# Two input tiles of expert 16 in a place of their own, and the output biases' products inside expert 0

## The chip, the cores and the metric

One core of one Trainium2 chip. The metric is the device time in microseconds (us) of one execution of the whole program, the median over several runs.

## The reference

Two blocks run in a row on 256 tokens of width 1024, all in fp32. The first (two layers of convolution, latent attention and dilated attention) and the attention of the second are untouched by the change. The second block ends in a mixture of experts, and this is what the change touches:

```python
logits = xt @ w_router + b_router
top_val, top_idx = lax.top_k(logits, TOP_K)          # 4 of 32 experts for each token
gates = softmax(top_val)
# for each expert e and the tokens that chose it:
hcat = xb @ w_in[e] + b_in[e]                        # 1024 x 2048
x_glu = minimum(hcat[:, :D_FF], 7.0)
x_lin = clip(hcat[:, D_FF:], -7.0, 7.0)
act = x_glu * sigmoid(1.702 * x_glu) * (x_lin + 1)
ys = act @ w_out[e] + b_out[e]                       # 1024 x 1024
# y[token] += gate * ys; then x + gt2 * y, and a last rms_norm
```

Each expert has 8 MB of input weights and 4 MB of output weights, and every expert's are read.

## The kernel before

**Stages.** The core runs the first block's two layers, then the second block's attention ("the block" below), then its output projection, the router, and the experts. Programs of the engines are written out by hand and meet in semaphores; each engine takes its own instructions in order, and every transfer is issued by SyncE (SP), in order, in `block_sync`.

**The ring.** Weights pass through a ring of six slots of 2 MB in SBUF. Each expert fills all six: tiles 0 to 3 are its input weights, 4 and 5 its output weights. Expert 0's are fetched during the block (4, 5, 3, 0 early; 1 and 2 once the last output projection unit is done). `expert(e, m)` in SP's loop over experts 1 to 31 refills a slot when TensorE has used the tile of the expert before: `mused` counts tiles 0, 1, 2 and 4, `lin_done` tile 3, `eout_done` tile 5 (L604 to L615). So up to six tiles are on their way.

**Between block and experts.** On VectorE (DVE): L1276 adds the output projection to x; L1286 clears seven buffers (`bin_sb`, `pos`, `ext`, `ys`, `spread`, `sel`, `selg`); `modulated` (L1132 to L1148) normalizes; then the router's choice, gates and places in each expert's list (L1291 to L1319); `select` (L1329) makes the one-hot matrices `sel` that gather the tokens of experts 0 and 1; then the job table (L1339 to L1355), a list of experts with more tokens than 64 slots, which is used only behind expert 31; and in each turn of the loop over pairs (L1391 on) first `onehots` (L1361, picks the expert's row of the input biases) and `gates_of` (L1368, gate masks). On TensorE (PE): sums of squares L812, router L819, four groups of transpositions of h to token order L830, places L835 to L839, gates turned L843, then eight products of the output biases and the gates into the four accumulating banks (L851), which wait for both bias tables (`bpar_loaded`), and `gather` of expert 0's and 1's tokens (L858) in two halves.

**The experts.** TensorE loops over 16 pairs of experts. For each of the two: `expert_in` (L869: products with tiles 0 to 3, and behind tile 1 the input bias L887), `turn_act` (L913), `expert_out` (L904: tiles 4, 5). In the pair's first expert eight `scatter` products (L927) add the pair before's rows into the banks, six ahead of `turn_act` and two behind; in the first pair they add zeros, as `ys` and `spread` were cleared. `turn_sel` (L920) turns the gate masks. In the pair's second expert the next pair's tokens are gathered. ScalarE (ACT) copies gathered and turned tiles out of PSUM (L1074, L1087, L1079); DVE clips and multiplies (L1375 to L1383) and copies the rows (L1388, L1389).

## Time and profile before

| | us |
|---|---|
| three runs | 2038.09, 2039.31, 2044.0 |
| median | 2039.31 |
| the profiled execution | 2037.97 |
| its span | 2036.2 |

| engine | busy us | share of the span |
|---|---|---|
| PE (TensorE, matmuls) | 1904.2 | 94% |
| DVE | 759.7 | 37% |
| ACT | 546.9 | 27% |
| POOL | 522.6 | 26% |

The mean rate of the DMA engines is 277 GB/s over the span; 563.19 MB are moved. A matmul record's end is modelled, so a busy PE is not PE at its peak, and a product in fp32 leaves two records. "Granted clock" is TensorE's clock as a share of its higher level: 1.00 is 2.4 GHz, 0.50 is 1.2 GHz. In a timeline, what stands in brackets behind a row is the engine's idle time ahead of it and what ended that.

### The profile page before, as it was taken

What the parts mean: (1) busy time and instruction counts of PE and PEld (TensorE: products, weight loads), DVE (VectorE), ACT (ScalarE), POOL (GpSimd) and SP (SyncE); (2) the same over time, 40 slices, a digit from 0 to 9 for tenths busy, and PEclk for the clock granted to TensorE, in tenths of its full rate; (3) what the DMA queues carried; (4) which work ended last, traced back from release to release, by engine and by line L of the source; (5) the groups of instructions that cost most, each with busy time, mean ns of one, the idle gap of its engine ahead of it and who ended that gap; (6) DMA issues with size and microseconds to landing.
All of it is one profiled execution on the core that took longest, in us unless ns stands there. A gap on an engine that the chain in (4) does not pass through costs nothing.

```text
span 2036.2 us, 26901 instructions
## 1 busy us (share of the span) xinstructions
PE 1904.2 (94%) x10970; PEld 1199.2 (59%) x10970; DVE 759.7 (37%) x1445; ACT 546.9 (27%) x922; POOL 522.6 (26%) x220
## 2 busy tenths in 40 slices
PE   7999999989999999799879999999999999999996
PEld 6779889977798899544465444333333333333433
DVE  4784643448836533734544111111111111111112
ACT  4554455445544554222411000000000000000001
POOL 5776656866755567000000000000000000000000
PEclk9999999999999999899998999999999999999999
DMA  8555333565543335421725999999999999999994
GB/s 297 200 183 176 125 125 125 172 231 176 201 150 130 120 125 189 158 75 42 287 93 208 430 428 428 430 428 429 428 428 429 428 428 429 429 429 428 428 429 193
DMA packets 111407, 563.19 MB, mean 277 GB/s; under 512 B 4768, under 2 KB 24352, under 8 KB 86464
## 3 DMA queue, kind: packets, MB, share of 16 engines
q1 hardware_dynamic: 111328, 562.09, 69.1%
q8 instruction: 56, 0.92, 0.2%
q14 instruction: 23, 0.19, 0.0%
HBM read 561.02 MB, written 1.05 MB: 276 GB/s over the span
## 4 chain that ended last, share of the span: by engine, by line
PE 57%; DMA 31%; DVE 7%; ACT 2%; issue 1%; SPq 0%; DVEq 0%; ACTq 0%
DMA ring<-in_e_in_dram 31%; PE bank L1595 14%; PE bank L1585 10%; PE score L869 9%; PE bank L695 4%; PE bank L1562 3%; PE mixed L904 2%; PE bank L802 1%; PE mixed L1679 1%; PE flip L1662 1%; DVE ring L2164 1%; PE score L1648 1%; PE flip L1620 1%; PE bank L927 1%; PE score L887 1%
## 5 line engine op out<-in xcount | busy, mean ns | idle before, releaser
L1971 POOL TENSOR_TENSOR w_lo<-ring,w_hi 128x1024 fp32r<-128x1024 f32 (+1 forms) x216 | 522.4, 2430 | 285.2 <-ACT w_hi L1873 284.6
L869 PE MATMUL score<-ring,space 128*64 128x512 f32 x2048 | 461.4, 595 | 46.2 <-DMA ring<-in_e_in_dram 45.2
L869 PEld LDWEIGHTS score<-ring,space 128*64 128x64 f32 x2048 | 142.3, 137 | 353.9 <-issue 246.2
L1873 ACT ACTIVATE w_hi<-ring 128x1024 fp32r<-128x1024 f32 (+1 forms) x216 | 226.3, 1049 | 221.5 <-PE bank L1595 122.5
L1595 PE MATMUL bank<-h_hi,w_hi 128*128 128x256 f32 x896 | 261.9, 292 | 0.0
L1595 PE MATMUL bank<-h_lo,w_hi 128*128 128x256 f32 x896 | 254.3, 284 | 0.0
L1595 PE MATMUL bank<-h_hi,w_lo 128*128 128x256 f32 x896 | 254.2, 284 | 0.0
L904 PE MATMUL mixed<-ring,space 128*64 128x512 f32 x1024 | 226.8, 595 | 0.0
L1083 ACT ACTIVATE space<-space 128x512 f32<-128x512 f32 x32 | 20.2, 631 | 718.9 <-DVE space L1375 718.9
L1375 DVE TENSOR_SCALAR space<-score 128x512 f32<-128x512 f32 x32 | 22.2, 694 | 431.7 <-PE score L869 431.7
L1595 PEld LDWEIGHTS bank<-h_hi,w_hi 128*128 128x128 f32 x896 | 172.8, 193 | 4.5 <-issue 4.4
L1595 PEld LDWEIGHTS bank<-h_lo,w_hi 128*128 128x128 f32 x896 | 172.7, 193 | 0.1
L1595 PEld LDWEIGHTS bank<-h_hi,w_lo 128*128 128x128 f32 x896 | 172.4, 192 | 0.0
L904 PEld LDWEIGHTS mixed<-ring,space 128*64 128x64 f32 x1024 | 70.7, 137 | 132.6 <-issue 130.6
L1585 PE MATMUL bank<-w_hi,h_hi 128*128 128x512 f32 (+1 forms) x320 | 131.4, 411 | 8.3 <-DVE h_lo L2027 8.3
L1388 DVE COPY space<-mixed 64x512 f32<-64x512 f32 x32 | 21.9, 685 | 295.6 <-PE mixed L904 295.6
L1585 PE MATMUL bank<-w_hi,h_lo 128*128 128x512 f32 (+1 forms) x320 | 124.9, 390 | 0.0
L1585 PE MATMUL bank<-w_lo,h_hi 128*128 128x512 f32 (+1 forms) x320 | 124.6, 389 | 0.0
L1585 PEld LDWEIGHTS bank<-w_hi,h_hi 128*128 128x128 f32 x320 | 61.0, 191 | 25.6 <-issue 12.5
L695 PE MATMUL bank<-ring,h 128*128 128x512 f32 (+1 forms) x160 | 66.6, 569 | 5.1 <-DVE h L1148 5.1
L1585 PEld LDWEIGHTS bank<-w_lo,h_hi 128*128 128x128 f32 x320 | 61.2, 191 | 11.7 <-issue 1.0
L1585 PEld LDWEIGHTS bank<-w_hi,h_lo 128*128 128x128 f32 x320 | 60.9, 190 | 12.0
(320 smaller groups left out, 2330.7 us busy)
## 6 DMA issues: line engine op xcount, KB each, us to landing
ring<-in_e_in_dram SPq DMA_DIRECT2D x128, 2048.0 KB, 25.2
ring<-in_e_out_dram SPq DMA_DIRECT2D x64, 2048.0 KB, 22.1
ring<-in_w_in_dram SPq DMA_DIRECT2D x42, 2048.0 KB, 7.8
ring<-in_w_ada_dram SPq DMA_DIRECT2D x16, 1024.0 KB, 5.4
ring<-in_w_o_dram SPq DMA_DIRECT2D x6, 2048.0 KB, 7.9
ring<-in_w_qkv_dram SPq DMA_DIRECT2D x4, 2048.0 KB, 9.9
ring<-in_w_ada_dram SPq DMA_DIRECT2D x4, 2048.0 KB, 8.0
ring<-in_w_out_a_dram SPq DMA_DIRECT2D x2, 2048.0 KB, 7.7
```

The source lines that it names most:

```text
L695: ins = pe.matmul(b[:, 0:n], src[:, c, tt * P:(tt + 1) * P], w8[:, c, 0:n], start=c == 0, stop=c == DC - 1)
L802: ins = pe.matmul(b[:, i * T:(i + 1) * T], w8[:, c, m:m + P], mix[:, c, :], start=c == 0 and i == 0, stop=c == DC - 1, skip_group_check=True)
L869: ins = pe.matmul(score[HALF * blk:HALF * blk + HALF, which * W:(which + 1) * W], xs[:, 2 * j + r, HALF * hh:HALF * hh + HALF], wk[:, blk ...
L887: pe.matmul(score[HALF * blk:HALF * blk + HALF, which * W:(which + 1) * W], onehot[:, hh, :], bin_sb[:, at:at + W], start=False, stop=False)
L904: ins = pe.matmul(mixed[HALF * side:HALF * side + HALF, :], actT[:, hh, a * P + HALF * half:a * P + HALF * half + HALF], ring[:, 4 + half, ...
L1375: dve.tensor_scalar(glu[:, hh, :], score[:, 0:W], GLU_LIMIT, None, ALU.min).then_inc(glu_free, 1)
L1388: dve.tensor_copy(ys[0:HALF, hh, :], mixed[0:HALF, :])
L1562: ins = pe.matmul(b[:, i * T:(i + 1) * T], w_[:, c, m], y_[br][:, c, :], start=c == 0 and i == 0 and y_ is y_hi and w_ is hi, stop=c == 3 ...
L1585: ins = pe.matmul(b[:, 0:n], x_[:, c, t], w_[:, k % PARTS, i, 0:n], start=c == 0 and x_ is h_hi and w_ is w_hi, stop=c == DC - 1 and x_ is ...
L1595: ins = pe.matmul(b[:, half * T:(half + 1) * T], w_[:, k % PARTS, i, m:m + P], x_[:, c, :], start=c == 0 and half == 0 and x_ is h_hi and ...
L1873: act.activation(split_part(w_hi, k), raw_part(k), ACT.Copy).then_inc(hi_done, 1)
L1971: pool.tensor_tensor(split_part(w_lo, k), raw_part(k), split_part(w_hi, k), ALU.subtract).then_inc(lo_done, 1)
```

## The change

Three things change. Line numbers are those of the kernel before.

1. **Parked tiles.** A place of two tiles (`parked_tiles`) is laid over h and the first 6144 columns of the work space. The buffers of the block and of the experts are moved so that nothing in use lies there. SP fetches tile 1 of expert 16 (the seventeenth) into it behind the last output projection unit, and tile 0 behind the fourth group of transpositions of h (L830), which reads h last. For expert 16 SP issues only tiles 2 to 5, and TensorE reads tiles 0 and 1 from there. SP's loop and TensorE's are split around it.
2. **Output biases.** The eight products of L851 become `bias_out` and stand in expert 0 where the scatter of zeros stood, which falls away, as do the clearing of `ys` and `spread`. The wait for the bias tables stands ahead of expert 0.
3. **Masks.** DVE makes `onehots` and `gates_of` of the first pair ahead of the job table. `jt`, `jt2` of the job table lie elsewhere.

```diff
@@ -188,6 +188,9 @@
+PARKED, NPARK = PAIRS, 2
+assert PARKED % 2 == 0
@@ -249,6 +252,8 @@
+        with nc.sbuf_tensor("parked_tiles", [P, NPARK, TILE], F32) as park:
+            pass
         h = sb("h", [P, DC, T])
...
@@ -601,10 +608,10 @@
-            def expert(e, m):
+            def expert(e, m, first=0):
                 we = e_in[bass.ds(e, 1)].rearrange("a k n -> (a k) n")
                 wo = e_out[bass.ds(e, 1)].rearrange("a k n -> (a k) n")
-                for j in range(MRING):
+                for j in range(first, MRING):
@@ -625,9 +632,21 @@
                 expert_tile(e_in[0], e_out[0], j)
             sp.wait_ge(mix_ready, 1)
             sp.dma_start(bout[0:NEXP, :], eb_out).then_inc(bpar_loaded, 16)
+            def park_tile(j):
+                sp.dma_start(park[:, j, :], e_in[PARKED].rearrange("(p j r) n -> p j (r n)", p=P, j=4)[:, j, :]
+                             ).then_inc(parked, 16)
+            sp.wait_ge(unit_done, bdone(NBU - 1))
+            park_tile(1)
             sp.wait_ge(table_ready, 1)
             sp.dma_start(bin_sb[0:NEXP, :], eb_in).then_inc(bpar_loaded, 16)
-            with sp.Fori(1, NEXP) as e:
+            sp.wait_ge(flipped, FLIP0 + F_TOK + 4)
+            park_tile(0)
+            with sp.Fori(1, PARKED) as e:
+                expert(e, e)
+            expert(PARKED, PARKED, NPARK)
+            with sp.Fori(PARKED + 1, NEXP) as e:
                 expert(e, e)
@@ -843,13 +862,14 @@
-            pe.wait_ge(mixed_free, MIXED0 + M_END + 1)
-            pe.wait_ge(bpar_loaded, 64)
-            for b in range(BANKS):
-                pe.wait_ge(bank_free[b], bfreed(NBU - BANKS + b))
-            for c in range(DC):
-                pe.matmul(bank[c // 2][:, (c % 2) * T:(c % 2 + 1) * T], bout[0:NEXP, c * P:(c + 1) * P],
-                          gateT[0:NEXP, :], start=c % 2 == 0, stop=False, skip_group_check=True)
+            def bias_out():
+                pe.wait_ge(mixed_free, MIXED0 + M_END + 1)
+                for b in range(BANKS):
+                    pe.wait_ge(bank_free[b], bfreed(NBU - BANKS + b))
+                for c in range(DC):
+                    pe.matmul(bank[c // 2][:, (c % 2) * T:(c % 2 + 1) * T], bout[0:NEXP, c * P:(c + 1) * P],
+                              gateT[0:NEXP, :], start=c % 2 == 0, stop=False, skip_group_check=True)
@@ -861,10 +881,12 @@
-            def expert_in(m, hh, biased):
+            def expert_in(m, hh, biased, here=False, behind=False):
                 def product(j, r, which):
-                    wk = ring[:, j, (2 * r + which) * D:(2 * r + which + 1) * D]
+                    tile_ = park[:, j, :] if here and j < NPARK else ring[:, j, :]
+                    wk = tile_[:, (2 * r + which) * D:(2 * r + which + 1) * D]
@@ -874,7 +896,10 @@
                 for j in range(3):
-                    pe.wait_ge(mlanded[j], m * 16 + 16)
+                    if here and j < NPARK:
+                        pe.wait_ge(parked, 16 * NPARK)
+                    else:
+                        pe.wait_ge(mlanded[j], m * 16 + (0 if behind and j < NPARK else 16))
@@ -935,20 +960,24 @@
-            with pe.Fori(0, PAIRS) as i:
+            def two_experts(i, first=False, here=False, behind=False):
                 pe.wait_ge(rows_in, i * 2 + 2)
                 pe.wait_ge(act_in, i * 2 + 1)
-                expert_in(i * 2, 0, i + 1)
+                expert_in(i * 2, 0, i + 1, here, behind)
                 pe.wait_ge(eout_free, i * 2 + 1)
-                pe.wait_ge(spread_in, i + 1)
-                scatter(range(0, 6))
+                if first:
+                    bias_out()
+                else:
+                    pe.wait_ge(spread_in, i + 1)
+                    scatter(range(0, 6))
                 turn_act(i * 2, 0)
-                scatter(range(6, DC))
+                if not first:
+                    scatter(range(6, DC))
                 turn_sel(i + 1)
                 expert_out(i * 2, 0)
-                expert_in(i * 2 + 1, 1, i + 1)
+                expert_in(i * 2 + 1, 1, i + 1, behind=here or behind)
...
+            pe.wait_ge(bpar_loaded, 64)
+            two_experts(0, first=True)
+            with pe.Fori(1, PARKED // 2) as i:
+                two_experts(i)
+            two_experts(PARKED // 2, here=True)
+            with pe.Fori(PARKED // 2 + 1, PAIRS) as i:
+                two_experts(i, behind=True)
@@ -1282,7 +1319,7 @@
-            for v in (bin_sb, pos, ext, ys, spread, sel, selg):
+            for v in (bin_sb, pos, ext, sel, selg):
@@ -1335,6 +1372,26 @@
+            def masks_of(i):
+                onehots(0, i * 2)
+                onehots(1, i * 2 + 1).then_inc(onehot_ready, 1)
+                gates_of(0, i * 2, lambda t: column(pos, t, i * 2))
+                gates_of(1, i * 2 + 1, lambda t: column(pos, t, i * 2 + 1)).then_inc(selg_ready, 1)
+            masks_of(0)
             for b in range(3):
                 ins = dve.tensor_scalar(cand0[:, b * NEXP:(b + 1) * NEXP], cnt, SLOTS * (b + 1) + 0.5, None, ALU.is_gt)
@@ -1354,21 +1411,6 @@
-            dve.wait_ge(bpar_loaded, 64)
...
@@ -1388,19 +1430,21 @@
+            two_experts(0)
+            with dve.Fori(1, PAIRS) as i:
+                base[0] = i * PER["pair"] + mark
+                steps[0] = 0
+                masks_of(i)
+                two_experts(i)
```

TensorE's program between the gate's transposition (L843, in the kernel after L862) and expert 0's output products, before:

```order
L843 MATMUL mixed<-cst,space 32x128 x2
L851 MATMUL bank<-space 128x256 x8
L858 MATMUL flip<-space 128x128 x8
L858 MATMUL score<-space 128x128 x8
...
L869 MATMUL score<-ring,space 64x512 x16
L883 REGISTER_ALU
L887 MATMUL score<-space 64x512 x4
L869 MATMUL score<-ring,space 64x512 x16
L927 MATMUL bank<-space 128x256 x6
L913 MATMUL score<-cst,space 128x128 x4
L927 MATMUL bank<-space 128x256 x2
L920 MATMUL flip<-cst,space 128x128 x4
L904 MATMUL mixed<-ring,space 64x512 x16
```

and of the change:

```order
L862 MATMUL mixed<-cst,space 32x128 x2
L878 MATMUL flip<-space 128x128 x8
L878 MATMUL score<-space 128x128 x8
L891 MATMUL score<-ring,space 64x512 x16
L912 MATMUL score<-space 64x512 x4
L891 MATMUL score<-ring,space 64x512 x16
L871 MATMUL bank<-space 128x256 x8
L938 MATMUL score<-cst,space 128x128 x4
L945 MATMUL flip<-cst,space 128x128 x4
L929 MATMUL mixed<-ring,space 64x512 x16
```

The output biases' products (`bank<-space 128x256 x8`, L851 and L871) went from ahead of the gathers (`flip<-space`, `score<-space` 128x128) to behind the input products, the place of the scatters (L927), of which none is left in expert 0.

SP's issues from expert 0's tiles to the first refills, before:

```order
L602 DMA ring<-in_e_out_dram 128x4096 x2
L602 DMA ring<-in_e_in_dram 128x4096 x4
L627 DMA space<-in_eb_out_dram 32x1024
L629 DMA space<-in_eb_in_dram 32x2048
L630 UNCONDITIONAL_BRANCH
L630 ISA
L602 ISA
L602 DMA ring<-in_e_in_dram 128x4096
```

and of the change:

```order
L609 DMA ring<-in_e_out_dram 128x4096 x2
L609 DMA ring<-in_e_in_dram 128x4096 x4
L634 DMA space<-in_eb_out_dram 32x1024
L636 DMA parked_tiles<-in_e_in_dram 128x4096
L643 DMA space<-in_eb_in_dram 32x2048
L636 DMA parked_tiles<-in_e_in_dram 128x4096
L646 UNCONDITIONAL_BRANCH
L646 ISA
L609 ISA
L609 DMA ring<-in_e_in_dram 128x4096
```

Two transfers to the parked place came in around the input biases' (`eb_in`); the loop of refills follows as before.

DVE's program from the end of the job table (L1354, L1355) into the loop over pairs, before:

```order
L1353 TENSOR_TENSOR space<-space,cst 128x1536
L1354 TENSOR_REDUCE space<-space 128x16
L1355 CAST space<-space 128x16
L1391 UNCONDITIONAL_BRANCH
L1391 ISA
L1361 COPY space<-cst 128x64
L1361 ISA
L1361 COPY space<-cst 128x64
```

and from the selections (L1366) on, of the change:

```order
L1366 TENSOR_SCALAR space<-cst,space 128x64 x4
L1376 COPY space<-cst 128x64 x2
L1383 TENSOR_SCALAR space<-cst,space 128x2x64 x2
L1383 TENSOR_SCALAR space<-cst,space 128x128 x2
L1396 TENSOR_SCALAR space<-space 128x32 x3
L1402 COPY space<-space 128x1
L1403 TENSOR_TENSOR space<-space 128x95
L1402 COPY space<-space 128x2
```

The one-hots (L1376) and gate masks (L1383) stand between the selections and the job table, which begins with L1396; before, they stood behind it, at the head of the loop.

## Rows read from the trace of the kernel before

**Rows 1.** The page: GB/s moved in 40 equal slices of the span

```profile
GB/s 297 200 183 176 125 125 125 172 231 176 201 150 130 120 125 189 158 75 42 287 93 208 430 428 428 430 428 429 428 428 429 428 428 429 429 429 428 428 429 193
```

**Rows 2.** Chain that ended last: start us, us, engine and group

```profile
1116.18 6.87 PE score L869 x32
...
1143.39 6.87 PE score L869 x32
...
1267.57 25.42 DMA ring<-in_e_in_dram
...
1972.39 25.43 DMA ring<-in_e_in_dram
```

**Rows 3.** Windows: length, PE busy us (records), granted clock, DMA share, GB/s

```profile
1060.00:1090.00 30.00, 21.90 (x93) 0.66 0.00 1
1114.00:1116.00 2.00, 2.00 (x12) 1.00 1.00 303
1120.00:1180.00 60.00, 59.77 (x298) 1.00 1.01 428
```

**Rows 4.** Timeline of SP: start us, us to the last, line, transfer

```profile
1044.63 0.80 SPq L602 DMA_DIRECT2D ring<-in_e_in_dram  x2
...
1092.83 12.34 SPq L602 DMA_DIRECT2D ring<-in_e_in_dram  x4
1113.02 4.08 SPq L602 DMA_DIRECT2D ring<-in_e_out_dram  x2
```

**Rows 5.** Timeline of PE, 1044 to 1097: start us, us, line, operation, records

```profile
1044.44 3.62 PE L812 MATMUL score<-h,ones 128*128 128x256 f32 x16
1055.60 5.37 PE L819 MATMUL mixed<-h,space 128*32 128x256 f32 x16 [7.54 <-DVE h L1148]
...
1067.48 1.12 PE L830 MATMUL flip<-cst,h 128*128 128x128 f32 x4 [1.12 <-ACT space L1064]
...
1074.85 7.19 PE L851 MATMUL bank<-space 32*128 32x256 f32 x16 [0.58 <-DVE space L1319]
1081.97 3.78 PE L858 MATMUL flip<-space 128*128 128x128 f32 x16
...
1088.93 7.09 PE L869 MATMUL score<-ring,space 128*64 128x512 f32 x32 [0.98 <-ACT space L1074]
```

**Rows 6.** Timeline of all engines, expert 0's middle, 1104 to 1117 us

```profile
1104.53 2.86 PE L927 MATMUL bank<-space 128*128 128x256 f32 x12
...
1107.89 0.60 ACT L1087 ACTIVATE space<-score 128x512 f32<-128x512 f32 x1 [3.61 <-PE score L913]
...
1109.09 7.09 PE L904 MATMUL mixed<-ring,space 128*64 128x512 f32 x32
```

**Rows 7.** DVE's groups by form, 1045.85 to 1050.4 us: busy us, mean ns

```profile
L1286 DVE MEMSET space<- 128x512 f32 x2 | 1.0, 485 | 0.1
L1286 DVE MEMSET space<- 128x1024 f32 x1 | 0.9, 912 | 0.2 <-issue 0.2
```

**Rows 8.** Timeline of DVE, 1050 to 1090 us

```profile
1050.64 0.42 DVE L1135 TENSOR_SCALAR space<-score 128x256 f32<-128x256 f32 x1
...
1074.72 0.73 DVE L1329 TENSOR_SCALAR space<-cst,space 128x64 f32<-128x64 f32 x4
...
1088.18 0.34 DVE L1361 COPY space<-cst 128x64 f32 x2 [0.35 <-DVE space L1355]
1088.52 1.12 DVE L1368 TENSOR_SCALAR space<-cst,space 128x128 f32<-128x128 f32 x4
```

**Rows 9.** Windows of PE: length, busy us (records), granted clock, DMA share, GB/s

```profile
1059.00:1060.00 1.00, 1.00 (x6) 0.92 0.00 0
...
1080.00:1081.00 1.00, 1.00 (x4) 0.50 0.00 0
...
1086.00:1087.00 1.00, 1.00 (x9) 0.76 0.00 0
```

**Rows 10.** DMA queues in 1120:1180: packets, MB, share

```profile
q8 instruction: 1, 0.02, 0.1%
```

More of the change, by code:

```diff
@@ L326, in build @@
         top[0] = phase0
+        ctx_x = take(DC, T)
+        bsquare = take(W)
+        kdup = take(2, 2 * HALF)
+        lamt = take(2, HALF)
+        assert DC * T + top[0] >= NPARK * TILE
         bpar = take(NBP)
@@ L329, in build @@
         brsx = take(T)
-        ctx_x = take(DC, T)
         assert top[0] <= phase0 + TT * MROPE + 24 * T
-        bsquare = take(W)
+        routed = top[0]
         bqn = take(2, W)
@@ L380, in build @@
         cand0 = take(96)
-        jt = take(MAXJOBS, 96)
-        jt2 = space[:, jt_at:jt_at + MAXJOBS * 96].rearrange("p (a b) -> p a b", b=96)
+        jt, jt2 = (space[:, jt_at + i * MAXJOBS * 96:jt_at + (i + 1) * MAXJOBS * 96].rearrange("p (a b) -> p a b", b=96)
+                   for i in range(2))
         jobe = take(MAXJOBS)
@@ L480, in build @@
         mlanded = [sem(f"mlanded{i}") for i in range(MRING)]
+        parked = sem("parked")
         mused = sem("mused")
@@ L969, in block_tensor @@
                     turn_sel(i + PAIRS + 1)
-                    expert_in(i + NEXP, 0, i + PAIRS + 1)
+                    expert_in(i + NEXP, 0, i + PAIRS + 1, behind=True)
                     turn_act(i + NEXP, 0)
@@ L1336, in block_vector, with onehots, gates_of @@
                 dve.sem_inc(s_, 1)
+            def onehots(hh, e):
+                return dve.tensor_copy(onehot[:, hh, :], ident[:, bass.ds(e, 1)].broadcast_to([P, SLOTS]))
+            def gates_of(hh, e, where):
+                for t in range(TT):
+                    quarters = selg[:, t, :].rearrange("p (a s) -> p a s", s=SLOTS)
+                    dst = quarters[:, 0::3, :] if hh == 0 else quarters[:, 1:3, :]
+                    ins = dve.tensor_scalar(dst, iota[:, 0:2 * SLOTS].rearrange("p (a s) -> p a s", s=SLOTS), where(t),
+                                            column(gate_half, t, e), ALU.is_equal, ALU.mult)
+                return ins
+            def masks_of(i):
[4 more added lines that the diff above has]
+            masks_of(0)
             for b in range(3):
```

27 lines of the change are left out of this document (5 added, 22 removed).

## Prediction

> **What bounds the kernel now.** I read the page's slices first, then the chain of waits, and then the timeline of the handover between block and experts. The slices [rows 1] show two halves: up to about 1070 us the DMA engines move 42 to 297 GB/s, and from the twenty-third slice on they stand at 428 to 430 GB/s until the last, in which the stream ends. The chain [rows 2] says the same of the end: from 1267.57 to 1972.39 us it is one pattern, seen 25 times: a ring tile takes 25.4 us to land, TensorE works on it, its slot is given back, and the next tile is issued. One period is (1972.39 - 1267.57) / 24 = 29.37 us, six tiles of 2 MB, so **4.89 us per tile**. Before 1260 us the chain runs over TensorE: experts 1 and 2 begin at 1116.18 and 1143.39, so 27.2 us each, less than the 29.4 us that the DMA engines need. TensorE is late at first and catches up; from then on it waits for data.
>
> So one stream sets the end: 31 experts of six tiles, with no hole once it is under way [rows 1, 3]. Its length is bytes over rate. Its start is TensorE's: the first refill of a ring slot is issued at 1092.83 us, one tile's work after expert 0 begins at 1088.93 [rows 4, 5]. Between 1060 and 1090 us the DMA engines move 1 GB/s [rows 3]. Two things pay then: fewer bytes in the stream, and an earlier expert 0.
>
> One more fact on the start. Of expert 1, tiles 0 to 3 are issued from 1092.83 us, and tile 4 at 1113.02, when TensorE has used expert 0's tile 4 [rows 4]. Four tiles take 19.6 us from the first bytes at about 1093.3, so the queue runs dry just then: the rate falls to 303 GB/s in 1114 to 1116 [rows 3]. Hence there is no cover in expert 0: each microsecond by which TensorE is earlier or later at its tile 4 is a microsecond of the end. The cover grows later, by 29.4 - 27.2 = 2.2 us per expert.
>
> **Part 1: two tiles parked.** Expert 16 takes its tiles 0 and 1 from a place of their own. The stream loses two tiles of 4.89 us, **-9.8 us**, if the transfers are free where they now stand and if the stream doesn't run dry at expert 16. The first: tile 1 is issued after the last output product, about 1045.9 us, behind two ring tiles issued from 1044.63 us on [rows 4] and the output biases, 128 KB; three tiles at 4.89 us end about 1060, when the lines are idle. The input biases, 256 KB, come behind it, at some 1063 us; TensorE now waits for them only ahead of expert 0, at 1088.93 [rows 5] or, by the sum below, 1081, still 18 us later. Tile 0 is issued when the last transposition to token order is done, now 1067.48 + 1.12 = 1068.6 [rows 5], and lands about 6 us later, ahead of the first refill. In SP's queue the next thing is a wait for TensorE's first tile, so nothing stands behind these two waits. The second: after expert 15's tile 3 lands (call it 0), four tiles are due in place of six. By TensorE's pieces (7.09 us for two input tiles' products and as much for two output tiles' [rows 5, 6], which leaves 27.2 - 3 x 7.1 = 5.9 for the bias products, gathers, scatters and turns) expert 15's output ends at about 15, parked tiles are used by 24, tile 2 (landed 14.7) by 28, tile 3 by 31, tiles 4 and 5 by 39 and 43. The refills of expert 17 are issued at those times and their turns in the stream come at 29, 34, 39, 44, 49 and 54. The narrowest margin is some 10 us, so the stream stays full; the 9.8 us that TensorE is then behind are made up at 2.2 us per expert within five of the fifteen that are left. Bounds: -9.8 and 0.
>
> **Part 2: fewer memsets.** ys (1024 wide) and spread (512 wide) are no longer cleared: 0.91 + 0.49 = **-1.40 us** [rows 7]. These stand on the path: TensorE's sums of squares end at 1048.06 [rows 5], and DVE gets to read them only at 1050.64, after the memsets [rows 8]; without them it reads at 1049.24, still after the sums. All behind it, through the router to the selections at 1075.45, moves with it. The granted clock could take part back: the router's products begin at 1055.60 [rows 5] and the clock rises from 0.50 to 1.00 in the microsecond from 1059 [rows 9], 3.5 us later; were the rise at the same moment, 1.4 us more of them would run at half rate, costing 0.7. Bounds -1.4 and -0.7.
>
> **Part 3: output biases behind the first input products.** The products of L851 hold TensorE from 1074.85 to 1082.04 us, and the gather of expert 0's tokens can't start before 1081.97, though its selections are ready at 1074.72 + 0.73 = 1075.45 [rows 5, 8]. Now the gather follows the selections: **-6.5 us**. Inside expert 0 they replace the scatter of zeros, 16 records of which 12 take 2.86 us at the full clock, so 3.8 [rows 6]; at 0.50 the bias products took 7.19 us, so at full clock about 3.6. All eight stand ahead of the transposition of the activations, where six scatter products of 2.86 us stood and two behind: they end at 1104.53 + 3.6 = 1108.1 in today's times, and ScalarE's copy of the turned activations, now at 1107.89 for 0.60 us, starts 0.9 later, at 1108.8, and ends at 1109.4; the output products start about there in place of 1109.09: **+0.4 us** [rows 6]. Bounds 0 and +0.8.
>
> **Part 4: masks ahead of the job table.** One-hots and gate masks cost DVE 0.34 + 1.12 = 1.5 us and go from behind the table, at 1088.18, to ahead of it [rows 8]. They follow the selections, so the gather doesn't wait for them; the table then ends at about 1087.9 less 1.4 plus 1.5, so some 1088, and the first work behind it is the clip of expert 0's gate half, which follows expert 0's input products: these end about 1104 now [rows 6], the gate half's about a microsecond and a half ahead, so 1095 then. 7 us of cover: nothing. If they stayed behind the table, the bias products of expert 0 would wait for the one-hots at about 1088, just where they would then begin: that is what the move avoids.
>
> **Part 5: the clock.** It is 0.50 through the gate's work and the bias products and rises at about 1086.5 us (0.76 over the microsecond from 1086) [rows 9]. The bias products ran 7.2 us without a gap in it, and it rose only 4.5 us after the gather began. If only the gather counts, its rise moves with it: 0. If the time that counts runs from the start of the bias products (11.6 us), the rise now comes 11.6 us after the gather's start: its second half costs 1.3 us more, and of expert 0's products 3 us run at half rate, 1.5 more: +2.8. The rise at 1059 came 3.5 us after products began [rows 5, 9], so I take the nearer end, **+0.8**. The Trainium skill, "TensorE: Matmul & The Clock Gate" (The HAM clock gate), says that the slow level is the default and that sustained matmul activity releases it. By that the bias products were part of the run-up and taking them away makes this term +2.8, which is rival (a); the row at 1080, still 0.50 behind 5 us of them, speaks for 0.
>
> **Code.** TensorE's loop over pairs becomes a first pair, a loop of seven, the ninth pair and a loop of seven. There is a code fetch in 1120:1180 already, with the lines full [rows 10], and TensorE is busy 59.77 of 60 us there [rows 3]. So 0.
>
> **Sum.** -9.8 - 1.4 - 6.5 + 0.4 + 0.8 = **-16.5 us**, against the profiled execution's 2037.97 us (span 2036.2 and 1.8 around it): **2021.5 us**. The median, 2039.31, is 1.3 above that execution; the sum on it would give 2022.8.
>
> **Rivals.** (a) *The clock rises late*: 2.8 in place of 0.8 us: 2023.5. For it: the bias products may have been part of what raised it, and the first rise behind the gather's start is the only one in the rows. Against it: 7 us of them alone raised nothing [rows 5, 9]. (b) *The earlier start is lost*: something else holds expert 0, such as the input biases landing later than 1089 us behind the parked tile, and parts 2, 3 and 5 give 0: 2037.97 - 9.8, about 2028. Against it: by part 1 they land some 18 us ahead of expert 0. (c) *The stream runs dry at expert 16* because TensorE, 9.8 us late, gives slots back too late, and the two tiles' gain is lost: 2037.97 - 6.7, about 2031. Against it: the margin of 10 us worked out above. (d) *Slower than before*: a code fetch at the new loop boundaries queues behind the ring tiles in flight. Five queued tiles are 24.5 us. A stop of that length at expert 16 finds a cover of about 10 and costs 14; a second, on entering the last loop, finds none and costs 20 or more: -16.5 + 14 + 20 = +17.5, 2055. It decides against the change once these stops sum to over 27 us, cover included. For it, the change adds three boundaries; against it the fetch in 1120:1180 [rows 10], for which TensorE did not stop. The Trainium skill, "Runtime: NRT & Kernel Launch" (Instruction fetch mechanics), says that a taken branch to a target out of reach forces a fetch before execution goes on. No row shows such a stop here; by that page's rule (d) is possible and no more. (e) *Neither part does what it says*, no change: 2038.
>
> Chances: forecast 0.68, (a) 0.12, (b) 0.07, (c) 0.07, (d) 0.04, (e) 0.02. The forecast's own range is 2018.5 (the clock stays up, 2 us better, and the terms' low ends) to 2025. To leave out no more than 2 in 10 the range takes in (a) and (b): **2018.0 to 2029.0**. A measurement of this kernel tells about 0.3%, 6 us, from no change; faster by more: forecast, (a), (b), (c): 0.94; within: 0.02; slower: 0.04.
>
> **What would show it.** In the profile after: two transfers to the parked place between 1045 and 1075 us; the gather right behind the selections at about 1074; the first refill at about 1085 in place of 1092.8; a rate of 428 GB/s through experts 16 and 17; TensorE busy without a wait for about five experts behind expert 16, then the 29.36 us pattern again; the last tile 3 landing near 1981 in place of 1972.39 + 25.43 = 1997.8 [rows 2]. Right in sum but wrong in parts: the start gains less and the clock's rise is later. Wrong: a hole in the DMA row at expert 16 or 17, a first refill later than 1088, or a TensorE idle time put down to issue at a loop's edge.

## The result, and the profile after

Four runs of the changed kernel have the median 2023.14 us (2021.89 to 2024.4); four of the kernel before, beside them, 2038.7 us. The ratio is 0.9923 with a 95% interval of 0.9911 to 0.9936: **15.7 us less** (13.0 to 18.1). The profiled execution took 2023.2 us with a span of 2021.4, 14.8 less than before's 2036.2.

The page's rates in 40 slices of the span after:

```profile
GB/s 300 196 181 187 125 126 126 173 207 202 184 170 126 126 126 154 187 84 42 225 194 242 427 428 429 428 429 428 429 429 428 427 429 428 429 429 427 429 429 184
```

Slices 20 and 21 now hold 225 and 194 GB/s in place of 287 and 93 [rows 1]: a part of the experts' weights moves there. The rate behind them is the same 428.

SP's issues (start, us to the last, line, transfer, count), to be read against [rows 4]:

```profile
1045.83 0.42 SPq L636 DMA_DIRECT2D parked_tiles<-in_e_in_dram  x1
1048.62 0.33 SPq L643 DMA_DIRECT2D space<-in_eb_in_dram  x1
1068.54 0.33 SPq L636 DMA_DIRECT2D parked_tiles<-in_e_in_dram  x1
1085.91 12.34 SPq L609 DMA_DIRECT2D ring<-in_e_in_dram  x4
1106.63 4.08 SPq L609 DMA_DIRECT2D ring<-in_e_out_dram  x2
```

Both parked transfers stand in the quiet stretch. They landed 16.8 and 7.2 us behind their issue, at 1062.6 and 1075.7, and the input biases 15.2 us behind theirs, at 1063.8, ahead of expert 0's start at 1082.02. The first refill is issued at 1085.91 in place of 1092.83, tile 4's at 1106.63 in place of 1113.02.

TensorE's timeline of the handover, against [rows 5, 6]:

```profile
1044.32 3.62 PE L831 MATMUL score<-h,ones 128*128 128x256 f32 x16
1053.87 6.21 PE L838 MATMUL mixed<-h,space 128*32 128x256 f32 x16 [5.93 <-DVE h L1185]
...
1062.93 1.11 PE L849 MATMUL flip<-cst,h 128*128 128x128 f32 x4 [1.12 <-ACT space L1101]
...
1075.51 3.75 PE L878 MATMUL flip<-space 128*128 128x128 f32 x16 [1.32 <-DVE space L1366]
...
1082.02 7.09 PE L891 MATMUL score<-ring,space 128*64 128x512 f32 x32 [0.74 <-issue]
...
1097.62 3.71 PE L871 MATMUL bank<-space 32*128 32x256 f32 x16
...
1102.70 7.09 PE L929 MATMUL mixed<-ring,space 128*64 128x512 f32 x32 [0.25 <-ACT space L1124]
```

The gather starts 1.3 us behind the gate's transposition and no longer behind the bias products, which now take 3.71 us inside expert 0 (1097.62). But the router's products (1053.87) took 6.21 us in place of 5.37, and a group of transpositions 1.11 in place of 0.66.

The clock (third number behind the window: busy us, records, granted clock), against [rows 9]:

```profile
1059.00:1060.00 1.00, 1.00 (x5) 0.93 1.15 492
...
1062.00:1063.00 1.00, 0.07 (x1) 0.78 0.28 57
...
1079.00:1080.00 1.00, 1.00 (x8) 0.69 0.00 0
1080.00:1081.00 1.00, 1.00 (x11) 1.00 0.00 0
```

It rose in the microsecond from 1059, as before, and fell to 0.50 in that from 1062 (0.78 is a fall at about 1062.6). It rose again at about 1079.6 (0.69 in the microsecond from 1079), 4.1 us behind the gather's start.

The chain of waits from expert 15 on (start, us, what), against [rows 2]:

```profile
1496.88 25.42 DMA ring<-in_e_in_dram
1522.35 3.68 PE score L891 x16
...
1537.76 6.87 PE score L891 x32
...
1634.73 24.59 DMA ring<-in_e_in_dram
...
1957.05 25.43 DMA ring<-in_e_in_dram
```

Here is the pattern that was to be seen: data set the pace up to expert 15's tile 3 (1522.35). Then the chain runs over TensorE until it gives back the slot of expert 19's tile 3 at 1634.73, and TensorE does not wait for data before expert 20's tile 3, which lands 24.59 us later: five experts without such a wait. From there it is data again. Windows of that stretch (length, PE busy, clock, DMA share, GB/s):

```profile
1106.00:1110.00 4.00, 4.00 (x20) 1.00 0.86 283
1500.00:1540.00 40.00, 37.88 (x192) 1.00 1.01 429
1540.00:1634.00 94.00, 93.77 (x458) 1.00 1.01 427
1640.00:1980.00 340.00, 318.79 (x1548) 1.00 1.01 428
```

TensorE is busy 93.77 of 94 us, and the rate stays at 427 to 429: no hole at experts 16 to 20. The one hole is at 1106 to 1110 (283). It is the hole of before at 1114 [rows 3], but deeper: the same four us behind the first refill, 1112.9 to 1116.9, held 352 GB/s before. The last tile 3 landed at 1957.05 + 25.43 = 1982.5.

### The profile page after: what moved, and what is told of

Its sections match the earlier page's. It is cut to its first block, busy times and chain, and to the rows that moved or that the text cites. A ratio compares the mean times of both kernels' runs of the same rounds, so it can differ in the third digit from the quotient of the medians.

```text
span 2021.4 us, 26833 instructions
## 1 busy us (share of the span) xinstructions
PE 1897.1 (94%) x10954; PEld 1196.2 (59%) x10954; DVE 759.4 (38%) x1443; ACT 546.9 (27%) x922; POOL 522.3 (26%) x220
## 4 chain that ended last, share of the span: by engine, by line
PE 61%; DMA 28%; DVE 7%; ACT 2%; issue 1%; SPq 0%; DVEq 0%; ACTq 0%
DMA ring<-in_e_in_dram 28%; PE bank L1639 14%; PE score L891 11%; PE bank L1629 10%; PE bank L714 4%; PE mixed L929 3%; PE bank L1606 3%; PE bank L821 1%; PE mixed L1723 1%; PE flip L1706 1%; DVE ring L2208 1%; PE bank L952 1%; PE score L1692 1%; PE score L912 1%; PE flip L1664 1%
## 5 line engine op out<-in xcount | busy, mean ns | idle before, releaser
L891 PE MATMUL score<-ring,space 128*64 128x512 f32 x2016 | 452.7, 594 | 38.7 <-DMA ring<-in_e_in_dram 38.0
L1120 ACT ACTIVATE space<-space 128x512 f32<-128x512 f32 x32 | 20.2, 631 | 710.0 <-DVE space L1417 710.0
L1430 DVE COPY space<-mixed 64x512 f32<-64x512 f32 x32 | 21.9, 685 | 296.2 <-PE mixed L929 296.2
## 6 DMA issues: line engine op xcount, KB each, us to landing
ring<-in_e_out_dram SPq DMA_DIRECT2D x64, 2048.0 KB, 22.1
```

Of the source, the lines that this page charges most:

```text
L891: ins = pe.matmul(score[HALF * blk:HALF * blk + HALF, which * W:(which + 1) * W], xs[:, 2 * j + r, HALF * hh:HALF * hh + HALF], wk[:, blk ...
L1430: dve.tensor_copy(ys[0:HALF, hh, :], mixed[0:HALF, :])
```

## Where the time went, counted from one point

The stretch ahead of the sums of squares (L812) is the same code in all kernels, but it ended between 1042.7 and 1048.3 us in the profiled executions. So all points below are counted from the start of the sums (1044.44 before, 1044.32 after). "Last issue" is the issue of expert 31's tile 3, the last transfer of the chain. Each row is one profiled execution (that of park_at_2 was the longest of its ten runs, 2037.28 us against a median of 2030.8); the last column is that of the timed runs against before's.

| kernel | gather | first refill | tile 4's refill | last issue | from it to the end | ratio of the runs (95%) |
|---|---|---|---|---|---|---|
| before | 37.5 | 48.4 | 68.6 | 927.95 | 63.8 | |
| after | 31.2 | 41.6 | 62.3 | 912.7 | 64.35 | 0.9923 (0.9911 to 0.9936) |
| park_only | 37.6 | 48.2 | 68.4 | 919.2 | 64.4 | 0.9960 (0.9945 to 0.9974) |
| bias_only | 31.15 | 41.6 | 62.4 | 922.0 | 65.4 | 0.9973 (0.9961 to 0.9984) |
| memset_back | 31.15 | 41.6 | 62.3 | 913.0 | 64.3 | 0.9935 (0.9918 to 0.9951) |
| masks_behind | 31.2 | 41.6 | 62.35 | 912.3 | 64.3 | 0.9924 (0.9907 to 0.9940) |
| park_at_2 | 30.2 | 40.9 | 64.5 | 921.7 | 65.4 | 0.9962 (0.9949 to 0.9974) |
| park_at_30 | 31.2 | 41.6 | 62.3 | | | 0.9962 (0.9949 to 0.9975) |
| keep_first | 29.1 | 40.5 | 62.4 | 912.5 | 64.4 | 0.9925 (0.9909 to 0.9942) |
| keep_all | 27.8 | 36.2 | 58.3 | 908.3 | 65.3 | 0.9905 (0.9888 to 0.9921) |
| split_bias | 30.2 | 41.0 | 60.3 | 911.2 | 65.5 | 0.9927 (0.9910 to 0.9944) |
| wide_bias | 27.8 | 36.2 | 56.8 | 907.55 | 65.7 | one run |
| combined | 27.8 | 36.2 | 55.5 | 907.2 | 62.6 | 0.9898 (0.9881 to 0.9914) |

For before to after this gives -6.3 at the gather, -6.8 at the first refill, -6.3 at tile 4's refill, -15.2 at the last issue and, with 0.5 back in the tail and 0.1 ahead of the sums, the 14.8 us of the spans.

## Experiments: the two gains apart

**park_only.** In the changed kernel, the bias products ahead of the gather again, the scatter of zeros and the memsets back, the masks behind the table:

```diff
+            pe.wait_ge(bpar_loaded, 64)
+            bias_out()
             pe.wait_ge(eout_free, 1)
...
-                if first:
-                    bias_out()
-                else:
-                    pe.wait_ge(spread_in, i + 1)
-                    scatter(range(0, 6))
+                pe.wait_ge(spread_in, i + 1)
+                scatter(range(0, 6))
...
```

> The change with its parts 2 and 3 undone: the output biases' products stand ahead of the gather again, the scatter of zeros is back in expert 0, the two memsets are back, the masks stand behind the job table. Only the two parked tiles (and the split loops) differ from the kernel before. Theory (the gains add: stream shorter by two tiles, start earlier by the bias products): first refill within 0.5 us of 1092.8, the last tile 3 lands 9.7 us earlier than before, span 2036.2 - 9.7 = 2026.5. Rival (the parked transfers or the code at the new loop edges cost something that the start hid in the change): 2028 or more, and a hole in the DMA rate at experts 16 to 18.

Measured: first refill at 48.2 from the sums (48.4 before), last issue 8.8 us earlier, span 2026.5, the median of the runs 2029.5. That the span is just the 2026.5 expected is luck: the sums began 1.5 us earlier than before's (1042.93) and the tail took 0.6 us longer. From the sums to the end the gain is 8.2 us, as by the ratio of the runs (0.9960). The chain before the parked expert lost 1.0 us against before's (from tile 4's refill to expert 15's issue 390.5 in place of 389.5), and across expert 16 it gained 9.6. That first stretch scatters between 389.5 and 390.5 in the kernels with the same data flow (bias_only 389.8, memset_back 389.6, combined 390.3), so nothing can be made of one microsecond there. The rate was 427 to 428 GB/s in 1500 to 1620 us, experts 15 to 19: the rival's hole is not there. No cost of the parked transfers or of the loop edges shows.

**bias_only.** In the changed kernel, no parked tiles and one loop of pairs 1 to 15; memsets kept:

```diff
-            with pe.Fori(1, PARKED // 2) as i:
+            with pe.Fori(1, PAIRS) as i:
                 two_experts(i)
-            two_experts(PARKED // 2, here=True)
-            with pe.Fori(PARKED // 2 + 1, PAIRS) as i:
-                two_experts(i, behind=True)
```

> The change without the parked tiles: bias products inside expert 0, masks ahead of the job table, one loop over pairs 1 to 15; the memsets of ys and spread are kept, so that they don't mix in. Theory (the start alone): gather at about 1075.6, first refill at about 1086, the tile 4 refill 6.4 us earlier than before, the stream's end 5.6 to 6.4 us earlier, span 2029.8 to 2030.6. The 0.8 us by which the stream fell behind its start in the change's trace should be here too if it comes from the first refills, and be absent (6.4 us gained, 2029.8) if it comes from the parked tiles. Rival (the two gains overlap, each alone is worth more than its part): under 2028.

Measured: gather at 31.15 in place of 37.5, tile 4's refill 6.2 us earlier, last issue 5.9 us earlier. The span, 2032.4, is off the expectation by 2, but not by this mechanism: the sums began 0.6 later than before's and the tail took 65.4 in place of 63.8 us. By the stages the gains are 8.8 and 5.9, together 14.7 against the 15.2 of both; by the runs the two ratios multiply to 0.9933, within the interval of the change. They add; neither rival holds. The other question of the expectation stays open: behind tile 4's refill 0.3 us were lost here, 0.8 in the change and 1.2 in park_only, all within that stretch's scatter.

## Experiments: the memsets and the masks

**memset_back.**

```diff
-            for v in (bin_sb, pos, ext, sel, selg):
+            for v in (bin_sb, pos, ext, ys, spread, sel, selg):
```

> The change with ys and spread cleared again (1.4 us of DVE work ahead of the normalization). Theory (the clock took the 1.4 us back: with the memsets gone the router's products begin earlier but run longer at 0.50, and the clock falls again ahead of the transpositions in place of behind them): selections ready at 1075.4 as in both traces, span within 0.3 us of 2021.4. Rival (the memsets are on the path and their removal is worth what it measures, while something else cost 1.4 us in the change): selections at 1076.8, span 2022.8.

Measured: gather at 31.15 from the sums (31.2 in the change), span 2021.4. Against the change's profile the memsets are worth nothing. Its timeline of TensorE shows how:

```profile
1055.23 5.46 PE L838 MATMUL mixed<-h,space 128*32 128x256 f32 x16 [7.54 <-DVE h L1185]
...
1061.75 0.66 PE L849 MATMUL flip<-cst,h 128*128 128x128 f32 x4
1063.53 0.66 PE L849 MATMUL flip<-cst,h 128*128 128x128 f32 x4 [1.12 <-ACT space L1101]
1065.31 0.69 PE L849 MATMUL flip<-cst,h 128*128 128x128 f32 x4 [1.12 <-ACT space L1101]
...
1075.23 3.12 PE L878 MATMUL flip<-space 128*128 128x128 f32 x13 [1.32 <-DVE space L1366]
```

The router's products begin 1.6 us later against the sums than in the change but take 5.46 in place of 6.21 us, and the transpositions stand 1.78 us apart at the higher clock, where the change has 2.24 at the lower. The clock took back what DVE saved. It need not take all: of the other executions without the memsets, masks_behind and park_at_30 have the gather at 31.2 too, but park_at_2 and split_bias at 30.2, and there the first three groups of transpositions stand 1.78 us apart at the higher clock (park_at_2: 1065.04, 1066.82, 1068.60). So leaving them out is worth 0 to 1.0 us, by where the clock falls.

**masks_behind.** The first pair's masks behind the job table again:

```diff
-            masks_of(0)
             for b in range(3):
...
             dve.sem_inc(table_ready, 1)
+            masks_of(0)
```

> The change with the first pair's one-hots and gate masks behind the job table again. Theory (they have room there too): the table ends at about 1087.5, the one-hots at 1087.9, and expert 0's input bias products, which need them, stand at 1088.9: no wait, span within 0.3 us of 2021.4. Rival (the move is needed, as the prediction said): the bias products wait, 0.5 to 2 us more.

DVE's timeline (start, us, line):

```profile
1086.71 0.17 DVE L1411 CAST space<-space 128x16 int32<-128x16 f32 x1
1087.03 0.30 DVE L1376 COPY space<-cst 128x64 f32<-128x64 f32 x2
...
1095.17 0.69 DVE L1417 TENSOR_SCALAR space<-score 128x512 f32<-128x512 f32 x1 [6.81 <-PE score L891]
```

The one-hots are made at 1087.03 + 0.30, and the input bias products (L912) that need them stand at 1088.07 with no wait. All points are those of the change. The move costs nothing and buys nothing.

## Experiments: where the parked tiles stand

**park_at_2, park_at_30.** Another expert is parked:

```diff
-PARKED, NPARK = PAIRS, 2
+PARKED, NPARK = 2, 2
```

and 30 in the other (a loop with no turns is left out).

> The change with expert 2 in place of expert 16 parked. Theory (a refill needs TensorE to have given its slot back; TensorE is 9.8 us later against the stream behind the parked tiles and makes up 2.2 us per expert; up to expert 2 it has made up one or two experts' worth): the stream has holes of 5 to 8 us behind expert 2, span 2021.4 + 5 to 8 = 2026 to 2029. Rival (two tiles fewer are two tiles fewer wherever they stand): 2021.4.

> The change with expert 30 parked. Theory: the stream stays full and ends 9.8 us earlier, but TensorE, behind by the two tiles' products, has only expert 31 to make up 2.2 us, and TensorE ends the program. By its pieces (output of expert 29 ends 15 us behind its tile 3's landing, two experts of 27.2 follow: 70 us, against 64 if the data set the end) 5.7 us are lost: span 2027. Rival (two tiles fewer wherever they stand): 2021.4.

park_at_2, windows of PE (length, busy, clock, DMA share, GB/s):

```profile
1110.00:1118.00 8.00, 8.00 (x38) 0.95 0.59 203
1118.00:1126.00 8.00, 8.00 (x40) 1.00 0.77 330
1126.00:1132.00 6.00, 6.00 (x31) 1.00 0.48 175
1132.00:1140.00 8.00, 7.86 (x52) 1.00 0.93 393
1140.00:1150.00 10.00, 10.00 (x50) 1.00 0.93 364
```

TensorE is busy throughout and the data have holes: 203, 330, 175 GB/s. From tile 4's refill to the last issue it took 857.3 us, 6.85 more than the change's 850.4. (Another 2.2 us came ahead, in expert 0, from a fall of the clock, below.) The median of the runs is 2030.8.

park_at_30, chain of waits (start, us, what):

```profile
1906.64 25.42 DMA ring<-in_e_in_dram
1932.10 3.68 PE score L891 x16
...
1967.54 7.02 PE mixed L929 x32
...
2003.27 3.74 PE bank L952 x16
```

Data set the pace to expert 29's tile 3 (1932.10); from there TensorE alone, to the last scatter 71.2 us later, where the pieces gave 70. In the change the last scatter starts 955.1 us behind the sums, here 960.5: 5.3 us lost, against an expected 5.7. The span, 2026.4, was helped by sums that began 1.5 us earlier; the median of the runs is 2031.2. So two tiles fewer are worth some 9 us only where TensorE has caught up enough before, and has experts enough behind.

## Experiments: the clock

**keep_first, keep_all.** Products of constants in TensorE's gaps, into a bank that the bias products overwrite:

```diff
+            def keep_on(n):
+                for _ in range(n):
+                    pe.matmul(bank[0][:, 0:T], ones, c_("mask")[:, 0:T], start=True, stop=True)
+
+            pe.wait_ge(bank_free[0], bfreed(NBU - BANKS))
+            keep_on(11)
```

and in keep_all also `keep_on(2)` behind three groups of transpositions, `keep_on(5)` behind the places' products, `keep_on(2)` behind the gate's.

> The change with eleven products of constants (128 x 256, written to a bank that is overwritten later) on TensorE between the sums of squares and the router's products, where it idles 6 us and its clock falls to 0.50. Theory (the clock fell because TensorE idled): clock 1.00 when the router's products begin, which end about 2.4 us earlier (about 1057.7 in place of 1060.1), as DVE's second group of chunks then sets their end; what is left of that at the gather depends on when the clock falls behind it: 0.5 to 2.5 us gained, span 2019 to 2021. Rival (the clock doesn't follow this gap, or the products delay the router's): 2021.4 or more.

> As keep_first, with such products also in the other gaps up to the gather: two behind each of the first three groups of transpositions, five behind the places' products, two behind the gate's transposition. Theory: clock 1.00 from the sums to expert 0; the router ends 2.4 us earlier, the transpositions take 1.3 less, the places' products 0.7 less, the gather 1.7 less: about 6 us, span 2015.4; in parts less where a filling product delays the real one by up to 0.4 us each. Rival (the fillers delay as much as the clock gives): 2020 to 2022.

keep_first, TensorE:

```profile
1046.40 4.91 PE L836 MATMUL bank<-cst,ones 128*128 128x256 f32 x22
1052.49 1.89 PE L844 MATMUL mixed<-h,space 128*32 128x256 f32 x8 [1.18 <-DVE h L1191]
1055.15 1.91 PE L844 MATMUL mixed<-h,space 128*32 128x256 f32 x8 [0.78 <-DVE h L1191]
...
1061.69 1.11 PE L855 MATMUL flip<-cst,h 128*128 128x128 f32 x4 [1.12 <-ACT space L1107]
...
1072.03 3.76 PE L884 MATMUL flip<-space 128*128 128x128 f32 x16 [1.32 <-DVE space L1372]
```

The router's products now come in two halves of 1.9 us at the higher clock, each on DVE's chunks, and end 1.6 us earlier against the sums (14.1 us behind their start in place of 15.8), with the first of them at the same point, 9.55. The clock falls again at 1061.2, the third group of transpositions takes 1.11, and 2.1 us of gain are left at the gather, 1.1 at the first refill, none at tile 4's. The span, 2019.8, lies in the expected range only because the sums began 1.4 us earlier than the change's; the last issue is 0.2 earlier and the median of the runs 2022.97, beside 2023.14. keep_all holds 1.00 all the way to expert 0: gather 3.4 us earlier than in the change, first refill 5.4, as the gather's two halves take 2.02 and 1.95 us in place of 3.75 and 2.23. That is nearly the 6 expected. But at tile 4's refill only 4.0 are left. The windows of expert 0 (length, busy, records, clock) show where it goes:

```profile
1095.00:1096.00 1.00, 1.00 (x8) 1.00 0.92 393
1096.00:1097.00 1.00, 0.95 (x6) 0.54 1.12 475
1097.00:1098.00 1.00, 1.00 (x4) 0.50 0.88 377
...
1099.00:1100.00 1.00, 1.00 (x6) 0.75 1.11 475
```

TensorE is busy, and yet the clock goes to 0.50 in the microsecond from 1096. What stands ahead of it are the eight bias products, from 1091.61 to 1095.33, so it falls 0.75 us behind them (not the 1.2 us that the expectation of wide_bias, below, gives). In keep_first the same happens at 1098.7, with the bias products at 1095.13 to 1098.85, in park_at_2 at 1104.0, with them from 1101.02 on. In the profiles of the change, bias_only, memset_back, masks_behind and park_at_30, which have the same eight products in that place, it doesn't: three executions of eight. The last issue comes 4.4 us earlier than the change's; the median of the runs, 2019.31, is 3.8 us less, and none of the four is as long as the change's shortest.

**wide_bias.** In keep_all, the bias products left out and eight products of constants over 128 rows in their place:

```diff
-                    pe.matmul(bank[c // 2][:, (c % 2) * T:(c % 2 + 1) * T], bout[0:NEXP, c * P:(c + 1) * P],
-                              gateT[0:NEXP, :], start=c % 2 == 0, stop=False, skip_group_check=True)
+                    pe.matmul(bank[c // 2][:, (c % 2) * T:(c % 2 + 1) * T], ones,
+                              c_("iota")[:, 0:T], start=c % 2 == 0, stop=False, skip_group_check=True)
```

> As keep_all, but the eight products of the output biases (over 32 rows of both operands) are replaced by eight products of constants over 128 rows, of the same 128 x 256 shape and at the same place; the output biases are left out. In keep_all the clock fell to 0.50 some 1.2 us behind these products, with TensorE busy all the time. Theory (the products over 32 rows made it fall): clock 1.00 through expert 0, first refill to tile 4's refill 20.7 us in place of 22.1. Rival (it falls for another reason, such as the long run at 1.00 before): 22.1 again.

```profile
1091.03 3.72 PE L881 MATMUL bank<-cst,ones 128*128 128x256 f32 x16
1094.59 0.64 PE L948 MATMUL score<-cst,space 128*128 128x128 f32 x4
...
1095.91 7.09 PE L939 MATMUL mixed<-ring,space 128*64 128x512 f32 x32 [0.25 <-ACT space L1134]
```

Same place, same 3.72 us, but the clock is 1.00 in every window from 1086 to 1112, the transposition behind takes 0.64 us and the output products 7.09 in place of 8.46. First refill to tile 4's refill: 20.5 us, expected 20.7. The last issue is 0.8 us earlier than in keep_all. This fits the theory and does not prove it. It is one execution, and the bias products themselves let the clock be in five of eight; and the products differ in their values too, constants in place of biases and gates. What speaks more plainly is the start: ahead of the gather 7.2 us of the bias products left the clock at 0.50 in before [rows 5, 9] and in park_only, and it rose 4.5 us behind the gather's start in both; where the gather follows with none of them ahead, it rose 4.1 to 6.2 us behind.

## Experiments: expert 0, and a kernel that is faster than both

**split_bias.** Four bias products where all eight stand, four behind expert 1's input products:

```diff
-                    bias_out()
+                    bias_out(range(0, 4))
...
                 expert_in(i * 2 + 1, 1, i + 1, behind=here or behind)
+                if first:
+                    bias_out(range(4, DC))
```

> The change with the output biases' products in two halves: four where all eight stand, four behind expert 1's input products. Theory (no cover in expert 0: what TensorE saves ahead of its tile 4 is saved at the end; the first half still fills the 2.2 us in which TensorE waits for DVE's activations): tile 4's refill 1.2 to 1.5 us nearer to the first refill than the 20.7 us of the change, the stream's end as much earlier, span 2020.0. Rival (the stream's own rate sets the end from the first refill on): 2021.4.

Tile 4's refill came 19.3 us behind the first in place of 20.7: the 1.4 us expected. From the first refill to the last issue it took 870.15 us, against 871.1 in the change. That looks like 1.0 of the 1.4, but masks_behind and memset_back, with all eight in one place, took 870.7 and 871.4. The span, 2019.4, had 1.6 us from earlier sums, and the runs don't show a gain: 0.9927 beside 0.9923.

**combined.** keep_all, the split, and in the gap ahead of the last sums of squares:

```diff
+            for _ in range(8):
+                pe.matmul(flip[:, 0:T], ones, c_("mask")[:, 0:T], start=True, stop=True)
             for c in range(DC):
```

> keep_all with the split of split_bias, and eight products of constants in the gap between the last scatter and the last sums of squares, where the clock fell to 0.50. Theory: expert 0's clock stays at 1.00 (half as long a run of products over 32 rows) and tile 4's refill comes 2.5 to 2.9 us earlier against the sums than in keep_all; the last sums take 3.6 us in place of 6.4; together 4 to 5.5 us: span 2017.3 - 5 = 2012. Rival (the clock falls in expert 0 all the same, and the tail is set by DVE and ScalarE): 2015 to 2017.

```profile
1993.66 3.72 PE L962 MATMUL bank<-space 128*128 128x256 f32 x16 [1.50 <-DVE space L1445]
1997.22 3.62 PE L1027 MATMUL flip<-cst,ones 128*128 128x256 f32 x16
2001.26 3.72 PE L1031 MATMUL score<-h,ones 128*128 128x256 f32 x16 [0.42 <-ACT h L1162]
```

The median of its runs is 2016.57 us, ratio 0.9898 (0.9881 to 0.9914), span 2013.9: the fastest of all, 6.6 us under the change by the medians. The two intervals just touch (the change's begins at 0.9911), but its longest run, 2019.73, is under the change's shortest, 2021.89. The clock stays at 1.00 in expert 0, tile 4's refill comes 2.8 us earlier than in keep_all, and the last sums take 3.72 us, where they took 5.41 in the change and 6.4 in keep_all. Expected were 4 to 5.5 us over keep_all; 3.4 came. The rest is missing at the last issue: only 1.1 of the 2.8. Against keep_all 0.6 us of it went before expert 15's tile 3, and 1.1 across expert 16, which gained 8.5 us here against 9.6 there, with no hole in the rate; why isn't known.

## Why the prediction was right, step by step

**The forecast** of 2021.5 us, 16.5 under its own profiled execution, stands against 2023.2 for the profiled execution after (14.8) and 2023.14 for the median (15.6 under the median before). The case that it called likeliest is the one that happened. The terms:

- **Two parked tiles, -9.8.** Across expert 16 the chain gained 9.7 us between before and after, 9.6 with park_only. But other kernels that park the same tiles gained less there, memset_back 8.8 and combined 8.5. From tile 4's refill to the last issue the gain is 8.95 between before and after, and 8.5 to 9.7 over the six kernels with the same work there (850.0 to 850.8 us, against 859.4 and 859.7 without parking). So the size is nearly that of two transfers, a little under 9.8. Landing times were told within 3 us, and the five experts of catching up are the rows from 1522.35 on. The margin that it worked out is shown from both sides by park_at_2 and park_at_30.
- **The memsets, -1.4: wrong, it is 0.0 here and at best -1.0.** The step that failed is the sentence that all behind the memsets moves with them, through the router to the selections. DVE was 1.7 us earlier at the router (1053.87 against 1055.60, 0.1 of it from ahead), and 0.1 us was left at the selections (1074.64 against 1074.72). The prediction had the mechanism as a bound, 0.7 back at the router; 0.8 came back there. It had no step for what is next: the clock fell at about 1062.6, ahead of three groups of transpositions in place of behind them, for another 0.8. memset_back shows it undone.
- **The bias products, -6.5: measured -6.3 to -6.4 at the gather.** The gather follows the selections as told (1075.51 behind 1075.36).
- **Inside expert 0, +0.4:** the refills of the first tile and tile 4 are 20.7 us apart in place of 20.2, so +0.5.
- **The masks, 0:** right in size. The sentence that the products would otherwise wait was wrong: masks_behind has 0.7 us to spare.
- **The clock, +0.8: measured -0.5 here.** From the gather's start to expert 0's it took 6.51 us in place of 6.96; the clock rose 4.1 us behind the gather in place of 4.5. The other kernels without bias products ahead of a gather at 0.50 took 6.5 to 7.5 us, so the sign is that of this execution. The rise came at most 6.2 us behind the gather, never the 11.6 of rival (a), which falls: the bias products ahead had been no part of what raised the clock. What the prediction didn't see is that the clock can fall behind them where they now stand.
- **Code at the loop edges, 0:** no stop of TensorE in the rows; from 1085 to 1957 us its longest wait is 1.0 us, for data.
- **Left out:** the tail took 0.5 us more. Of that 0.2 is behind the start of the last sums, which ran longer at 0.50 (5.41 us in place of 5.25; up to 6.7 in others). The other 0.37 lies between the last scatter and these sums, before and after:

```profile
2022.01 5.25 PE L980 MATMUL score<-h,ones 128*128 128x256 f32 x16 [3.50 <-ACT h L1111]
...
2007.04 5.41 PE L1017 MATMUL score<-h,ones 128*128 128x256 f32 x16 [3.88 <-ACT h L1148]
```

  From the scatter's start to that of the sums it is 7.23 us before and 7.59 to 7.61 in all twelve other kernels. It stands on DVE, whose first addition behind the scatter comes 1.62 us behind its memset (in all twelve, within 0.01) in place of 1.25, with no wait that the profile shows. So this is a small cost of what all twelve have in common against before; which part of it wasn't tried.

The forecast was too good by 1.4 (memsets), 0.9 (parked tiles), 0.2 (bias products), 0.1 (expert 0) and 0.5 (the tail, left out), and too bad by 1.3 (clock) and 0.1 (ahead of the sums): 1.7 us in all. That the errors partly cancel is luck.

**The rule that the prediction cited.** The row of before had spoken against counting the bias products as part of what raises the clock, and the rises above bear it out. The Trainium skill, "TensorE: Matmul & The Clock Gate" (The HAM clock gate), has the clock follow how busy TensorE has been. By the windows of keep_all it fell to 0.50 with TensorE busy 1.00, and in wide_bias, once, it stayed at 1.00 with other products of the same length. So busy time as the profile counts it does not foretell the clock here; the measurement decides.

**That each microsecond at TensorE's tile 4 is one of the end was too strong.** With the tile 4 refill 1.4 us later behind the first (keep_all, keep_first: 22 us) the last issue came 0.9 later behind the first refill; with it 1.4 earlier (split_bias, combined: 19.3) 1.0 and 0.2 earlier. Where the rest goes wasn't settled: executions of kernels with the same work there differ by up to 1 us.

## What to carry to other kernels

Where one stream of weights sets the end and the engine that uses them is somewhat faster, a tile fetched in a quiet stretch ahead is worth nearly its whole transfer time (here 8.95 of 9.8 us for two), but only for a consumer far enough from both ends of the stream: park it where the user has already caught up and can catch up again. Work that stands between the last input of the first consumer and that consumer costs the time by which it holds it up (here 6.3 of its 7.2 us), and can go into the first wait behind it. Time saved on another engine ahead of TensorE is worth nothing until the clock's rows have been read behind it; products of constants in the gaps kept 1.00 here up to expert 0 and took 3.8 us off the median (keep_all), more than the memsets' 0 to 1.0.

## What the runs showed of the hardware that was not expected

- TensorE's clock fell from 1.00 to 0.50 with the engine busy all the time, towards the end of 3.7 us of products over 32 rows or within 0.8 us behind them (keep_first, park_at_2, keep_all). In five other profiles with the full run it did not fall, nor with as long a run of products of constants over 128 rows (wide_bias) or half as long a run over 32 (combined, split_bias). These three are one execution each, so that the number of rows is the cause is likely but not shown, and what decides whether the fall comes is open. It stretched the time from the first refill to tile 4's from 20.7 us to 21.9, 22.1 and 23.6.
- The stretch ahead of the experts, the same code in all kernels, differed by up to 5.5 us between executions (sums of squares from 1042.7 to 1048.3 us), so that a span alone can't tell changes of 2 us apart; points counted from the sums agree within 0.1 us up to the first refill where the clock did the same, and within 1 us where it did not (the gather 30.2 to 31.2 us behind them in the kernels without fillers or bias products ahead of it).
